# A three-part layer stack on one core: transposed inputs from the host, paired index heads, narrow weight blocks in two chunks, paired rope heads, side stages set further apart

## The reference, cut to what matters

```python
# first layer, twice (SEQ = 256, D_MODEL = 2048, 4 branches of width 512, heads of 128)
h = rms_norm(x, norm_g);  u = h @ w_in          # 2048 x 15944
a: index scores  sum_h w_h * relu(qi_h . ki)    # 8 index heads of 64; top 64 of the keys per query
   then softmax attention over the chosen keys
b: retention (rope on q and k, decay table);  c: gated linear recurrence (hgrn2)
m: attention over mem @ w_mem_kv (256 memory rows)
x = x + (sum_n sigmoid(gate_n) * ((y_n * silu(z_n)) @ w_branch[n])) @ w_out
# second layer, once
q = rms_norm(c_q) @ w_uq          # 8 heads, each 128 plain ("nope") + 64 with rope
kv = rms_norm(c_kv) @ w_ukv;  k_rope: one key of 64 shared by all heads
score = (q_nope . k_nope + q_rope . k_rope) * 192**-0.5      # branch l, softmax, times v
d: three dilated band attentions mixed, 8 heads of 128
x = x + (g0 * y_l + g1 * y_d) @ w_o
x = x + (silu(gt) * up) @ w_down          # D_FF = 5632
```

## Time and profile before

| | |
|---|---|
| median of three runs | 3365.7 us (3364.85 to 3367.43) |
| the profiled execution's own time | 3367.36 us |
| its span | 3365.6 us |
| TensorE busy | 3334.4 us, 99% |
| VectorE / ScalarE / GpSimd busy | 57% / 45% / 8% |
| chain that ended last | PE 97% |
| granted TensorE clock, mean | 0.998 |
| HBM traffic | 183 GB/s over the span |

### The profile page before, as it was taken

The page is one execution under the profiler, slowest core; times in us unless marked ns, Lnnn a source line. Parts: engine busy times, 40 slices in busy tenths (PEclk is TensorE's granted clock), DMA queues, the critical chain, the costliest instruction groups (busy, mean ns, idle before and its releaser), DMA issues.

```text
span 3365.6 us, 39487 instructions
## 1 busy us (share of the span) xinstructions
PE 3334.4 (99%) x15388; PEld 2755.9 (82%) x15388; DVE 1905.1 (57%) x2078; ACT 1517.1 (45%) x1926; POOL 278.2 (8%) x235
## 2 busy tenths in 40 slices
PE   8999999999999999999999999999999999999999
PEld 7888888888888788888888888887888888888887
DVE  5475655555555656555555555564555555555555
ACT  5444445444444444454444445454444444444443
POOL 0010240000000102310000011150000000000000
PEclk9999999999999999999999999999999999999999
DMA  7655555666666555555766675554565666666665
GB/s 266 182 169 167 165 170 168 198 196 194 188 198 197 170 163 169 169 169 173 215 194 188 196 210 168 151 181 126 171 198 186 188 189 192 190 190 191 191 191 168
DMA packets 321304, 617.96 MB, mean 184 GB/s; under 512 B 25056, under 2 KB 25440, under 8 KB 319968
## 3 DMA queue, kind: packets, MB, share of 16 engines
q1 hardware_dynamic: 321120, 615.45, 61.1%
HBM read 608.03 MB, written 7.34 MB: 183 GB/s over the span
## 4 chain that ended last, share of the span: by engine, by line
PE 97%; ACT 1%; DVE 1%; issue 1%; DMA 0%; SPq 0%; ACTq 0%; DVEq 0%
PE G L861 90%; PE PT L635 3%; PE PO L735 1%; PE PS L718 1%; ACT w_hi L875 1%; PE PS L696 1%; PE PS L762 0%; PE PS L761 0%; DVE w_lo L1103 0%; PE PS L720 0%; DMA arena<-in_mem 0%; PE G L855 0%; PE PS L784 0%; ACT core L1006 0%; DMA raw<-in_w_in 0%
## 5 line engine op out<-in xcount | busy, mean ns | idle before, releaser
L1103 DVE TENSOR_TENSOR w_lo<-raw,w_hi 128x1024 fp32r<-128x1024 f32 (+2 forms) x1150 | 1411.2, 1228 | 1412.7 <-ACT w_hi L875 1395.5
L875 ACT ACTIVATE w_hi<-raw 128x1024 fp32r<-128x1024 f32 (+2 forms) x1150 | 1199.1, 1044 | 1717.6 <-PE G L861 1698.8
L861 PE MATMUL G<-w_hi,xh 128*128 128x512 f32 x3200 | 1271.8, 397 | 2.8 <-DVE w_lo L1103 2.8
L861 PE MATMUL G<-w_hi,xl 128*128 128x512 f32 x3200 | 1248.1, 390 | 0.0
L861 PE MATMUL G<-w_lo,xh 128*128 128x512 f32 x3200 | 1245.8, 389 | 0.0
L861 PEld LDWEIGHTS G<-w_hi,xh 128*128 128x128 f32 x3200 | 601.2, 188 | 128.0 <-issue 10.5
L861 PEld LDWEIGHTS G<-w_hi,xl 128*128 128x128 f32 x3200 | 600.7, 188 | 128.6
L861 PEld LDWEIGHTS G<-w_lo,xh 128*128 128x128 f32 x3200 | 601.7, 188 | 118.9
L861 PE MATMUL G<-w_hi,yh 128*128 128x512 f32 x1304 | 517.5, 397 | 3.0 <-DVE w_lo L1103 3.0
L861 PE MATMUL G<-w_hi,yl 128*128 128x512 f32 x1304 | 510.3, 391 | 0.0
L861 PE MATMUL G<-w_lo,yh 128*128 128x512 f32 x1304 | 510.1, 391 | 0.0
(11 more groups left out here) (134 smaller groups left out, 1404.5 us busy)
## 6 DMA issues: line engine op xcount, KB each, us to landing
raw<-in_w_in SPq DMA_DIRECT2D x624, 512.0 KB, 3.7
raw<-in_w_gate_up SPq DMA_DIRECT2D x176, 512.0 KB, 3.7
raw<-in_w_down SPq DMA_DIRECT2D x88, 512.0 KB, 3.6
raw<-in_w_branch SPq DMA_DIRECT2D x64, 512.0 KB, 3.9
raw<-in_w_out SPq DMA_DIRECT2D x64, 512.0 KB, 4.5
raw<-in_w_mem_kv SPq DMA_DIRECT2D x32, 512.0 KB, 4.9
raw<-in_w_o SPq DMA_DIRECT2D x32, 512.0 KB, 3.6
raw<-in_w_o_dil SPq DMA_DIRECT2D x16, 512.0 KB, 3.6
```

What stands on the lines that cost most here:

```text
L861: mm = M.matmul(G[b % 2][:, t, 0:blk.width], a[:, blk.kk + k, tok], w[:, c % RING, j, 0:blk.width], start=(k == 0 and q == 0), stop=(k == ...
L875: A(w_hi[:, c % RING, :, 0:blk.width], raw[:, c % RING, :, 0:blk.width], ACT.Copy).then_inc(hi_done, 1)
L1103: V.tensor_tensor(w_lo[:, c % RING, :, 0:w], raw[:, c % RING, :, 0:w], w_hi[:, c % RING, :, 0:w].bitcast(F32), ALU.subtract).then_inc(lo_d ...
```

## The change

1. `mem` and `x` also come transposed from the host (`mem_by_col`, `x_by_col`). The first two activation feeds (`mem_feed`, `x_feed` of the first layer) need no TensorE: ScalarE and VectorE split the transposed rows directly (`mem_high/mem_low` chunk by chunk along the first block, `first_high/first_low`). The memory arrives in eight loads of 256 KB, each ahead of its weight chunk, in place of four of 512 KB; the identity, `x` and the tables come later.
2. Narrow blocks are cut into 2 chunks of 8 slices (24 matmuls each) instead of 8 chunks of 2 slices. There are 1132 chunks now.
3. Index heads go in pairs: one 128-wide transpose turns two heads, the key is copied twice side by side before its turn, and a stage does four matmuls, even head on rows 0 to 63 into `PS`, odd head on rows 64 to 127 into `PO`. 4 `rel` stages a layer instead of 8.
4. The rope parts of `w_uq` are put behind the plain parts by the host, so that two heads' rope parts (128 columns) are turned at once, every other head. The key is laid out between zeros (`kr_spread`) and turned twice, so that the rope matmul has 128 rows, half of them zero.
5. The table of stages: in `soft`, `s_pt` goes from c + 5 to c + 6, `s_pv` from c + 7 to c + 8, `tail` from c + 9 to c + 11 or c + 12. Heads of branch l stay 4 chunks apart, heads 4 to 7 of branch d go from 5 to 4 apart. The first `s_turn` of branch d comes 3 chunks after `h_sum` of its key (before: 6), that of head 4 also 3 (before: 5).
6. ScalarE does the sigmoid of a "bias" block after the side stages of that chunk, not ahead of them. Two memsets on GpSimd are added for the zeros.

```diff
+        self.ck = CK if width == NB else kt // 2
-        return self.kt // CK
+        return self.kt // self.ck
@@ soft
-        at(c + 5, "s_pt", br, l, h)
-        at(c + 7, "s_pv", br, l, h)
-        at(c + 9, "tail", br, l, h)
+        at(c + 6, "s_pt", br, l, h)
+        at(c + 8, "s_pv", br, l, h)
+        at(c + (11 if br in "dl" else 12), "tail", br, l, h)
@@ schedule
+    for i in range(KD // CK):
+        at(9 + 2 * i, "first_feed", i)
-        soft(r + (25 + 5 * h if h < 4 else 44 + 5 * h), "d", 2, h)
+        soft(r + (22 + 5 * h if h < 4 else 45 + 4 * h), "d", 2, h)
-        soft(r + 97 + 4 * h, "l", 2, h)
+        soft(r + 91 + 4 * h, "l", 2, h)
@@ TensorE, index scores and rope part
-                for j in range(2):
-                    mm = M.matmul(PS[:, j * T:(j + 1) * T], qi_t[:, 2 * p + j, t * P:(t + 1) * P], ki_t, start=True, stop=True)
+                for t in range(TT):
+                    for j, out_j in enumerate((PS, PO)):
+                        half_j = slice(j * IDX_DIM, (j + 1) * IDX_DIM)
+                        mm = M.matmul(out_j[:, t * T:(t + 1) * T], qi_t[half_j, p, t * P:(t + 1) * P], ki_t[half_j, :], start=True, stop=True)
-                        mm = M.matmul(PS[:, t * T:(t + 1) * T], qr_t[:, t * P:(t + 1) * P], kr_t, start=False, stop=True)
+                        mm = M.matmul(PS[:, t * T:(t + 1) * T], qr_t[h // 2 % 2][:, t * P:(t + 1) * P], kr_t[h % 2], start=False, stop=True)
@@ TensorE, chunks
+                    if blk.name == ("mk", 0):
+                        pe.wait_ge(mem_fed, s + 1)
+                    if blk.name == ("a_qi", 0):
+                        pe.wait_ge(first_fed, s + 1)
@@ ScalarE and VectorE, first block
+            def mem_high(i):
+                act.wait_ge(mem_in[i], 16)
+                A(yh[:, CK * i:CK * (i + 1), :], mem_t[:, CK * i:CK * (i + 1), :], ACT.Copy).then_inc(mem_hi, 1)
+            def mem_low(i):
+                dve.wait_ge(mem_hi, i + 1)
+                k = slice(CK * i, CK * (i + 1))
+                V.tensor_tensor(yl[:, k, :], mem_t[:, k, :], yh[:, k, :].bitcast(F32), ALU.subtract).then_inc(mem_fed, 1)
@@ ScalarE, order within a chunk
+                    later = ended is not None and BLOCKS[ended].kind == "bias"
+                    if ended is not None and not later:
+                        read_out(ended)
                     if c >= RING:
                         between(c - RING)
+                    if later:
+                        read_out(ended)
```

More of the change, by code:

```diff
@@ L139, in soft @@
         at(c + 2, "s_qk", br, l, h)
[L140 to L142 removed]
+        at(c + 6, "s_pt", br, l, h)
+        at(c + 8, "s_pv", br, l, h)
+        at(c + (11 if br in "dl" else 12), "tail", br, l, h)
     for n in range(4):
[L145 to L150 removed]
+        at(16 + 4 * n, "x_sq", 0, n)
+    for i in range(KD // CK):
+        at(9 + 2 * i, "first_feed", i)
     for l in range(DEPTH):
@@ L233, in numbered @@
     return out
-FEEDS = ("mem_feed", "x_feed", "m_feed", "l_feed", "h_feed")
-PT_OF = numbered(lambda s: 2 if s[0] == "ki" or s[:2] == ("s_turn", "l") else int(s[0] in FEEDS + ("qi", "s_turn", "s_pt", "tail", "c_f", "c_q", "b_turn", "kr", "back")))
+FEEDS = ("x_feed", "m_feed", "l_feed", "h_feed")
+PT_OF = numbered(lambda s: 2 if s[:2] == ("s_turn", "l") and s[3] % 2 == 0 else int(s[0] in FEEDS + ("qi", "ki", "s_turn", "s_pt", "tail", "c_f", "c_q", "b_turn", "kr", "back")))
 HI_OF = numbered(lambda s: int(s[0] in FEEDS + ("tail",)))
@@ L240 @@
 PO_OF = numbered(lambda s: int(s[0] in ("s_pv", "c_pv", "b_pv")))
+FIRST_PO = [PO_OF["s_pv", "a", l, 0] for l in range(DEPTH)]
 Y_OF = numbered(lambda s: int(s[0] in ("s_pv", "norm")))
@@ L255, in need @@
 def need(name, s):
-    if name == ("mk", 0):
-        return {0: ("mem_feed", 1, 1), 4: ("mem_feed", 2, 1), 6: ("mem_feed", 3, 1)}.get(s)
-    for first, e in ((("a_qi", 0), 0), (("a_qi", 1), 1), (("qd0", 2), 2), (("gt", 0), 3)):
+    for first, e in ((("a_qi", 1), 1), (("qd0", 2), 2), (("gt", 0), 3)):
         if name == first:
@@ L710, in s_turn @@
                 turn(i, [(q(t), t * P) for t in range(TT)] + [(k(t), (2 + t) * P) for t in range(TT)])
-                if br == "l":
-                    turn(i + 1, [(q2[:, t, h * QW + NOPE:(h + 1) * QW], t * P) for t in range(TT)])
+                if br == "l" and h % 2 == 0:
+                    turn(i + 1, [(q_rope[:, t, h * ROPE2:(h + 2) * ROPE2], t * P) for t in range(TT)])
             def s_qk(s, br, l, h):
-                turned(pe, PT_OF["s_turn", br, l, h] + (br == "l"))
+                turned(pe, PT_OF["s_turn", br, l, h] + (br == "l" and h % 2 == 0))
                 ps_turn(s)
@@ L729, in po_turn @@
                     pe.wait_ge(y_ready, o)
+                if o in FIRST_PO:
+                    pe.wait_ge(ps_free, PS_OF["rel", FIRST_PO.index(o), 3] + 1)
             def weigh(o, v):
@@ L794, in between @@
                     what, *args = stage
-                    if what == "mem_feed":
-                        mem_feed(PT_OF[stage], *args)
-                    elif what == "x_feed":
+                    if what == "x_feed":
                         x_feed(PT_OF[stage], *args)
@@ L836, in between @@
                         pe.wait_ge(rope2_ready, 1)
-                        turn(PT_OF[stage], [(krn[:, t, :], t * P) for t in range(TT)])
-            pe.wait_ge(ident_in, 16)
-            between(-1)
+                        turn(PT_OF[stage], [(kr_spread[:, t, (1 - i) * ROPE2:(3 - i) * ROPE2], (2 * i + t) * P) for i in range(2) for t in range(TT)])
             for b, blk in enumerate(BLOCKS):
@@ L1019, in between @@
                     what, *args = stage
-                    if what == "mem_feed":
-                        high_two(PT_OF[stage], yh, 4 * args[0] + 2 * args[1], None, 0)
+                    if what == "first_feed":
+                        first_high(*args)
                     elif what == "x_feed":
@@ L1313, in between @@
                     what, *args = stage
-                    if what == "mem_feed":
-                        low_two(stage, yh, yl, 4 * args[0] + 2 * args[1], None, 0)
+                    if what == "first_feed":
+                        first_low(*args)
                     elif what == "x_feed":
@@ L1486, in _ @@
             x_norm(2)
+            for i in range(2):
+                link(V.memset(kr_spread[:, :, 2 * i * ROPE2:(2 * i + 1) * ROPE2], 0.0))
             for q in range(2):
```

238 lines of the change are left out of this document (136 added, 102 removed).

## The result

| | before | after |
|---|---|---|
| median of 4 runs | 3365.5 us (3364.9 to 3367.4) | 3338.4 us (3337.0 to 3339.0) |
| profiled execution, own time | 3367.4 us | 3337.0 us |
| its span | 3365.6 us | 3335.2 us |

The ratio is 0.9916, 95% interval 0.9903 to 0.9928: 27.1 us less. The forecast was 3341 (3329 to 3354), faster at 93%. The profiled execution was the shortest of the four and that of the kernel before the longest; between them lie 30.3 us, where the steps gave 24.3.

The account below looks back on a forecast made before the run. The prediction took TensorE, busy 99% of the span, to bound the kernel. Gains of 50.5 us less costs of 26.2 gave net 24.3, so 3365.7 - 24.3 = 3341.4, rounded to 3341 us, range 3329 to 3354.

Parts of the forecast that it names:

- Start: First weight matmul 6.1 us earlier, at 8.3, and 16 `mem_feed` transposes saved (1.8 us): 8.0 us gained together.
- `x_feed`: First layer's feed of `x`: 8 stages of four TensorE transposes go, 3.5 us gained.
- Fewer transposes elsewhere: Index heads 32 to 16, rope queries 16 to 8, key +2: 22 fewer transposes, 2.4 us gained.
- `PS` in branch l: New TensorE wait of 2.3 us for VectorE's reciprocal before the scores of heads 1 to 7: 16.1 us lost.
- The rival that it costs nothing: Branch l's `PS` wait is free because VectorE runs far enough ahead: 3318 us; chance 5%.
- The clock behind it: Half-clock stretches follow four of branch l's seven new pauses, 1.7 us each: 6.8 us lost.
- the clock holds: Rival: no fall to half clock behind branch l's new pauses: 3334 us; chance 15%.
- Index scores: 8 paired stages replace 16, halves overlapping but for one more step: 7.5 us gained, plus 0.8 for 8 fewer returns.
- The upper bound: Index stages' two array halves run wholly side by side: 9.2 us gained.
- Scores of branch l: With 128 rows throughout, a head's scores go from 2.40 to 1.54 us: 6.9 us gained, plus 0.8 for 8 returns.
- First turns of branch d: New TensorE wait for GpSimd's key product at first `s_turn` and at head 4, 1.65 us each: 3.3 us lost.
- Waits that go: TensorE waits in narrow blocks (2.8 us) and other places (12.7), and three half-clock stretches (5.1), vanish: 20.6 us gained.

Follow-up runs that it names:

- experiment 1: Changed kernel with branch l's `s_pt` back at c + 5 and `s_pv` at c + 7, one chunk before the next scores: 3323.0 us.
- experiment 6: Changed kernel with the rope matmul reading only its own 64 rows, so 128-row and 64-row matmuls alternate in branch l: median 3357.0 us, ten executions 3349.5 to 3367.5.
- experiment 7: experiment 2 with the rope matmul also on its own 64 rows, as in experiment 6: 3335.8 us, one execution.
- experiment 5: Changed kernel with both matmuls of an index stage's even head issued before the two of the odd head, not by turns: 3338.2 us.
- experiment 8: Changed kernel with four `mem` loads (1 MB) issued ahead of the first weight load, ScalarE waiting for all four: 3345.1 us, one execution.
- experiment 2: experiment 1 with ScalarE doing a bias block's sigmoid ahead of its chunk's side stages again: 3325.5 us.
- experiment 10: experiment 1 with the rope matmul on its own 64 rows, as in experiment 6: 3329.4 us.
- Experiment 9: experiment 1 with narrow blocks cut into 8 chunks again and later stages of the table moved 6 chunks on behind each: 3336.7 us.
- experiment 3: Changed kernel with the old distances in all branches: `s_pt` at c + 5, `s_pv` at c + 7, `tail` at c + 9: 3325.4 us.

## Why the prediction was right, and where it was not

The sign, the size and most of the terms were right, because each edit was read as a shift of TensorE's own time and the new wait was found in the order of VectorE's work. That the total came so near is in part luck, for some terms put the gain 10.9 us too low and others 4.1 too high. Against the profiled execution (24.3 forecast, 30.3 found):

- *Start*: 8.0, found 7.9. *`x_feed`*: 3.5, found 3.9: a stage cost 0.48 us, not 0.44 (0.36 between the chunks and 0.12 in the steps of the chunk behind it).
- *Fewer transposes elsewhere*: 2.4, not timed by itself; the 86 records fewer are the 64 of the first two feeds and these 22.
- *`PS` in branch l*: 16.1, found 15.4 waited, and about as much given back when it was undone (experiment 1). The rival that it costs nothing is refuted, by the row it was argued from: the split in front of the reciprocal needs the chunk to be over.
- *The clock behind it*: 6.8, found 0. This is the step that failed. I took the share of falls from the earlier trace rows, where pauses of this size were followed by half clock, and let their length decide; the matmuls around them were named but given no price. Two of the three falls there stood near scores of mixed rows, which the same change removes. In the profiled executions, pauses of 2.2 to 2.3 us in branch l were followed by a fall in 10 of 10 cases with mixed rows (before 2, experiment 6 seven, experiment 7 one) and in 2 of 22 with 128 rows (after 7, experiments 5 and 8 seven each, experiment 2 one). That is no law: experiment 6's trace is its longest execution, and its shortest had room for two or three falls. And 14 of the 22 are fewer than they seem: the seven pauses of the changed kernel and of experiment 5 come within 0.2 us of the same moments. The rival "the clock holds" (3334, 15%) is what the profiled execution shows; the other three took 1.3 to 2.0 us more at a mean clock of 0.999, the size of one fall, but have no trace, so whether a fall was in them isn't shown. The median, 3338.4, lies between that rival and the forecast.
- *Index scores*: 7.5 + 0.8, found 16 x 1.15 - 8 x 1.155 = 9.1, and 1.0 of returns. The upper bound was the truth; experiment 5 shows why.
- *Scores of branch l*: 6.9 + 0.8, found 6.2 (experiment 10): I charged the return to 128 rows as a gain, but the step behind the new stage is longer, not shorter.
- *First turns of branch d*: 3.3, found 2.1. Head 0 waited 1.5 as worked out; for head 4 GpSimd's product took 1.94 us, not the 2.90 of the earlier trace rows, and the wait was 0.6.

```profile
2133.63 1.94 POOL L1474 TENSOR_TENSOR arena<-arena,stat 128x1024 f32<-128x1024 f32 x1
```

- *`c_pv`*: 0, found 2.5. The narrow blocks move every later block by 6 chunks and the table moves the stages of branch c by 3; the prediction has no term for where a stage then meets the end of a block.
- *Waits that go*: the 2.8 us of the narrow blocks, the 12.7 of the other places and the three falls (5.1) are all gone, as forecast. Experiment 9 says that 2 chunks are worth more, 13.7, in the new table; for the 12.7, experiments 2 and 3 show the cause of 4.8 us only.

The differences, -0.1 + 0.4 + 0.7 + 6.8 + 1.8 - 1.5 + 1.2 - 2.5 = 6.8 us, against 6.0 found; the last 0.8 was not traced.

## What to carry over

When a stage is moved, ask not which chunk it lands on but what it lands beside: two stages of one chunk that share a buffer cost the whole chain that frees it, and a block that ends there brings its read-out with it. A chunk between them cost nothing here and gave back 15.4 us. Pauses of a bounding engine should be priced with the clock as a spread rather than a number, and with what the engine does around them.
